# A two-block transformer kernel on one core: three activation tensors that TensorE reads as moving operands start 32, 224 and 96 bytes further on in SBUF

## The reference

```python
# first block, once
u = rmsnorm(h); q, k, v, g_ret, lru_in, lru_gate, gate_a, gate_b = split(u @ w_in)
y_ret = (silu(g_ret) * retention(q, k, v)) @ w_branch_ret
r = rg_lru(causal_conv(lru_in), ...)              # the recurrence
y_lru = (gelu(lru_gate) * r) @ w_branch_lru
h = h + (sigmoid(gate_a) * y_ret + sigmoid(gate_b) * y_lru) @ w_out
h = h + (silu(g) * up) @ w_ffn_out; h = rmsnorm(h)
# second block, once
o_gla, o_dsa, o_mem = gated_linear_attention(..), sparse_attention(..), memory_attention(..)
merged = gate0 * (o_gla @ w_o_gla) + gate1 * (o_dsa @ w_o_dsa) + gate2 * (o_mem @ w_o_mem)
x = x + merged @ w_out
x = x + hierarchical_moe(rmsnorm(x))
```

## The kernel before

| product | moving, its start | stationary, its start | distance |
|---|---|---|---|
| lru, dsaT, memoT, ret, normedT by weights, 256 columns | 64 | 128 | 192 |
| xT by weights, 256 columns | 64 | 128 | 192 |
| glaT by weights, 256 columns | 192 | 128 | 64 |
| xT by weights, 272 columns | 0 | 128 | 128 |
| weights by mixed, 512 columns | 128 | 128 | 0 |
| weights by hidden, 512 columns | 128 | 64 | 64 |
| pick by zrows, 256 columns | 64 | 64 | 0 |
| normedT by the small weights swhi and swlo, 256 columns, slice k | 64 | 96 and 224, plus 432 k | changes with k |

## Time and profile before

### The profile page before, as it was taken

One profiled execution on the slowest core, in us unless ns is written; L12 is line 12 of the kernel. 1 busy time (PEld: TensorE's weight loads), 2 busy tenths in 40 slices (PEclk: granted clock), 3 DMA queues, 4 the chain that ended last, 5 costly groups with the idle time before them and its releaser, 6 DMA issues.

```text
span 1092.3 us, 17231 instructions
## 1 busy us (share of the span) xinstructions
PE 1078.8 (99%) x7088; PEld 965.0 (88%) x7088; DVE 730.3 (67%) x817; ACT 625.7 (57%) x751; POOL 48.6 (4%) x43
## 2 busy tenths in 40 slices
PE   9999999999999999999999999999999999999997
PEld 7998889999889999998898768899999978888885
DVE  6944675865765454455775649975454778998885
ACT  7653369664465444444574446855444567877773
POOL 0600100000000000000000000000000000000140
PEclk9999999999999999999999999999999999999999
DMA  8552254654646555554446333253446547999991
GB/s 312 194 193 77 79 193 155 249 192 141 249 159 222 199 192 187 196 193 155 157 170 213 116 116 129 103 193 116 168 166 220 200 186 259 331 374 350 340 347 78
DMA packets 30786, 214.84 MB, mean 197 GB/s; under 512 B 3424, under 2 KB 3680, under 8 KB 5248
## 3 DMA queue, kind: packets, MB, share of 16 engines
q1 hardware_dynamic: 28400, 199.35, 51.3%
q0 software_dynamic: 1904, 13.14, 3.2%
q10 hardware_dynamic: 416, 1.40, 0.3%
HBM read 212.82 MB, written 1.05 MB: 196 GB/s over the span
## 4 chain that ended last, share of the span: by engine, by line
PE 95%; DVE 3%; ACT 1%; DMA 0%; issue 0%; DVEq 0%; SPq 0%; ACTq 0%
PE bank L565 28%; PE bank L567 28%; PE bank L566 28%; PE bank L626 2%; PE bank L1037 1%; PE bank L1114 1%; PE bank L959 1%; PE bank L941 1%; DVE wlo L1690 1%; DMA buf<-x_dram 0%; PE bank L707 0%; PE bank L872 0%; PE bank L1091 0%; PE bank L704 0%; PE bank L868 0%
## 5 line engine op out<-in xcount | busy, mean ns | idle before, releaser
L1690 DVE TENSOR_TENSOR wlo<-raw,whi 128x2048 fp32r<-128x2048 f32 x138 | 317.8, 2307 | 168.0 <-ACT whi L1149 167.7
L1149 ACT ACTIVATE whi<-raw 128x2048 fp32r<-128x2048 f32 (+1 forms) x168 | 319.3, 1906 | 131.0 <-PE bank L567 127.2
L565 PE MATMUL bank<-normedT_hi,whi 128*128 128x256 f32 x640 | 177.6, 278 | 0.0
L566 PE MATMUL bank<-normedT_lo,whi 128*128 128x256 f32 x640 | 177.0, 277 | 0.0
L567 PE MATMUL bank<-normedT_hi,wlo 128*128 128x256 f32 x640 | 177.0, 277 | 0.0
L1149 ACT ACTIVATE buf<-bank 128x512 f32<-128x512 f32 (+5 forms) x147 | 71.0, 526 | 156.0 <-PE bank L567 127.2
L565 PE MATMUL bank<-xT_hi,whi 128*128 128x256 f32 (+1 forms) x448 | 127.1, 284 | 0.8 <-issue 0.8
L566 PE MATMUL bank<-xT_lo,whi 128*128 128x256 f32 (+1 forms) x448 | 126.4, 282 | 0.0
L567 PE MATMUL bank<-xT_hi,wlo 128*128 128x256 f32 (+1 forms) x448 | 126.4, 282 | 0.0
L565 PEld LDWEIGHTS bank<-normedT_hi,whi 128*128 128x128 f32 x640 | 120.1, 188 | 1.0 <-issue 0.6
L566 PEld LDWEIGHTS bank<-normedT_lo,whi 128*128 128x128 f32 x640 | 120.3, 188 | 0.7 <-issue 0.2
(11 more groups left out here) (406 smaller groups left out, 2260.1 us busy)
## 6 DMA issues: line engine op xcount, KB each, us to landing
raw<-weights_dram SPq DMA_DIRECT2D x168, 1024.0 KB, 4.9
buf<-weights_dram SPq DMA_DIRECT2D x19, 1024.0 KB, 6.9
buf<-x_dram SPq DMA_DIRECT2D x2, 512.0 KB, 4.4
buf<-mem_dram ACTq DMA_DIRECT2D x1, 1024.0 KB, 8.9
out_dram<-buf SPq DMA_DIRECT2D x4, 256.0 KB, 2.7
buf<-final_w_dram POOLq DMA_DIRECT2D x1, 512.0 KB, 4.1
con<-consts_dram SPq DMA_DIRECT2D x1, 486.0 KB, 9.3
buf<-small_w_dram SPq DMA_DIRECT2D x1, 432.0 KB, 11.8
```

Of the source, the lines that this page charges most:

```text
L565: E.matmul(out_, lh, rh, start=start, stop=False)
L566: E.matmul(out_, lh, rl, start=False, stop=False)
L1149: return S.activation(out_, in_, func, **kw)
L1690: V.tensor_tensor(wlo[:, n % SLOTS, :], raw[:, n % SLOTS, :], whi[:, n % SLOTS, :].bitcast(f32), sub).then_inc(piece_split, 1)
```

## The change

Each of the three pairs gets an offset `at`. lru starts 8 elements (32 bytes) further on, dsaT 56 elements (224 bytes), memoT 24 elements (96 bytes), hi and lo alike. Their starts modulo 256 become 96, 32 and 160, and the distances 224, 160 and 32, which are 7, 5 and 1 times 32. The buffers have 2176 elements and the tensors 2048, so the shifted tensors stay in their buffers. No instruction is added, removed or moved on any engine: the sequences of all five engines are the same in both programs, and so is every shape. The instructions that write these tensors and those that read them take other addresses.

```diff
@@ -369,7 +369,7 @@
         RG, IG, TH, AA, A2, HS = cols(7, TM), cols(9, TM), cols(8, TM), cols(10, TM), cols(11, TM), cols(7, TM)
-        LT, LTP = cols(13), pair("lru", 10, 11)
+        LT, LTP = cols(13), pair("lru", 10, 11, at=HELD // 2)
         GA, GB, RTP = cols(4), cols(5), pair("ret", 6, 7)
@@ -406,11 +406,11 @@
-        ODP = pair("dsaT", 9, 10)
+        ODP = pair("dsaT", 9, 10, at=3 * HELD + HELD // 2)
         MQR, MQT = rows(11), cols(12)
         MP = buf[8][:, 0:2048].rearrange("p (a c) -> p a c", a=4)
         MPT = buf[13][:, 0:2048].rearrange("p (h s t) -> p h s t", h=MH, s=2)
-        OMP = pair("memoT", 11, 12)
+        OMP = pair("memoT", 11, 12, at=HELD + HELD // 2)
```

## The result

The changed kernel takes 1096.79 us (median of 17 runs, 1094.47 to 1098.65); the kernel before, 17 runs beside them, takes 1094.1 us (1091.94 to 1095.14). The ratio is 1.0026, with a 95% interval of 1.0018 to 1.0035: 2.8 us slower, 2.0 to 3.8. The forecast was +2.6 us, given as 1095.9 us on the 1093.3 us of the first three runs, with a range of 1090.4 to 1097.6; on the 1094.1 us of the 17 runs it would be 1096.7.

What follows compares the result with a forecast made beforehand. TensorE was taken as the bound, busy 1078.8 of 1092.3 us. The terms 0 + 2.6 + 0 + 0 gave +2.6 us on 1093.3 us, so 1095.9 us (+0.24%), range 1090.4 to 1097.6.

Steps and rivals of the forecast that it cites:

- Step 1: 576 matmuls of lru, dsaT and memoT: streaming from the new distances costs 4.5 ns each, 2.6 us; chance 0.37.
- Stays at 113: Rival: the three stages keep 113 ns despite the new distances; 1093.3 us, 0.0%; chance 0.28.
- A start in the middle of 64 bytes costs extra: Rival for the changed matmuls: 120 to 121 ns each, +3.9 to +4.5 us; chance 0.19 for 119 ns and more.
- Faster: Rival: new starts avoid a clash of reads in the 576 matmuls; 2.7 to 3.7 us gained; chance 0.16, 0.08 over 3.3 us.
- The estimate of 109.2 ns: Skill's N/2.4 + 2.5 ns between 256-column matmuls, set beside the faster side; 2.3 us less if the new starts reached it.
- The skill's rule of two independent ports: TensorE reads moving operand and weight load through separate SBUF ports, so the change would be worth 0.
- Step 2: ScalarE and VectorE writing at the new starts: any change covered by 43, 78 and 75 us before TensorE reads; 0.
- Step 3: Stages behind move as a block, charged 0; gate2 keeping the slower pace would be 0.9 us more.

Runs made afterwards that it cites:

- Run 1: Kernel before plus 25 groups of 48 matmuls, 256 columns, at chosen distances between moving and stationary start; 1247.99 us, which measures nothing.
- runs 2 to 4: Changed kernel with distances exchanged, with even multiples, or with dsaT back at 192; 1098.26, 1096.19 and 1093.82 us, kernel before 1095.21.
- run 7: Kernel before plus groups with one column loaded repeatedly, 32 loaded columns, or 128 moving columns, at several distances; no total given, it is no measure.
- no_dsa: Changed kernel with dsaT put back to distance 192, lru and memoT still changed; 1093.82 us, one execution, kernel before 1095.21.
- paces_512: Kernel before plus 16 groups of 48 matmuls with 512 moving columns at the eight distances; no total given, it is no measure.
- entries: Kernel before plus groups at each distance, each followed by two at 192, then transposes followed by a group at 192; no total given.
- even: Changed kernel with even multiples: lru at distance 128, dsaT at 64, memoT at 0; 1096.19 us, one execution, kernel before 1095.21.
- turned_round: Changed kernel with distances exchanged: lru 160, dsaT 32, memoT 224; 1098.26 us, one execution, kernel before 1095.21.
- weights32: Kernel before with the weights' parts whi and wlo moved by 32 bytes, activations left alone; 1115.1 us against 1093.63, ratio 1.0192.
- best: Kernel before with hidden and memT products at distance 0 and one bf16 matmul ahead of gb.3 and br_lru; 1098.96 us against 1093.91, ratio 1.0044.
- hidden_0: Kernel before with hidden alone moved to distance 0; 1097.88 us against 1093.9, ratio 1.0037.

## Why the prediction was right

**Step 1, streaming from the new starts (+2.6 us).** Right in its mechanism and nearly in its size. The price was 4.5 ns, to 117.7, taken from ret, gla and gate0; the three stages measure 118.3, 117.3 and 116.7, mean 117.4, which over 576 matmuls is 2.4 us. Run 1 found the same three numbers with nothing else of the kernel in them, and runs 2 to 4 moved them between tensors. The prediction's own sentence, that right in kind and wrong in being one number is possible, applies. That the price came so near is in part luck: ret and gate0 lie at 192 and show its second pace, 117.8, which is no price of another distance. Of the three only gla is one.

**The rivals.** "Stays at 113" fell in all three stages. "A start in the middle of 64 bytes costs extra" fell in run 1, where moving both starts by 32 bytes changed nothing; its 120 ns belong to distances 0 and 96 and to the second pace of 128. The 120 ns that the small weights showed at 32 and 160, with 88 loaded columns and over a few matmuls, are 116.7 and 117.3 with 128 columns. "Faster" fell: 113.3 is the floor of every table for 256 columns. The estimate of 109.2 ns from the Trainium skill ("TensorE: Matmul & The Clock Gate", "Back-to-back issue gap") was not reached either; that section gives its formula for the gap of an isolated matmul and says that in a stream where each has its own load both set the pace, as they do here, so the estimate was no forecast for this stream. The skill's rule of two independent ports ("TensorE: Matmul & The Clock Gate", "Step-by-step: what each phase is for") would have made the change worth nothing; the runs decide against it here, for what is loaded (run 7: 113.3 or 116.7 ns at distance 192) and from where (run 1: 118.3 or 113.3 ns for the same moving start) changes the pace of the stream.

**Step 2, writing (0).** Right. The profile after has 2292, 682 and 692 ns for the lo parts, the durations of the earlier trace rows.

**Step 3, the stages behind (charged 0).** Wrong in that profile by the 0.9 us it named: gate2 kept a slower pace, 117.8, and *no_dsa* took that away again. It rested on the earlier trace rows, where 113 ns came back within three matmuls behind distance 64. That was one hand-over, not a rule; behind dsaT at 160 it didn't come back.

**Why the total still fits.** Step 1 was 0.2 us too high and step 3 0.8 us too low, so the nearness of +2.6 and +2.8 is luck as well. The steps measured add to 0.94 + 0.77 + 0.84 + 0.65 = 3.2 us, and the times show 2.8 (2.0 to 3.8). A part of the difference may be that lru's 113.3 before is itself a draw: of eight profiles in which it lies at 192 with nothing put ahead of it, two had it at 117.8 (*paces_512*, *entries*), so its mean price is (6 x 0.94 + 2 x 0.12) / 8 = 0.74 and the sum 3.0. That is worked out from eight profiles and not measured.

**What scatters the times.** One part is ret, which was at 117.8 in ten of the 13 profiles that have it at 192 and at 113.3 in three (the changed kernel, *even*, *paces_512*): 1 us. A larger part is the granted clock. Of the 17 executions of the changed kernel the four with a mean granted clock of 0.997 took 1097.4 to 1098.7 us, and the three with 1.0 took 1095.1 to 1096.2. Where a profile has such a stretch it is short and early. The windows from 100 to 140 us of the kernel before and of *turned_round*, whose 1098.26 us it lengthened:

```profile
100.00:140.00 40.00, 40.00 (x253) 33.80 (x253) 25.13 (x50) 17.81 (x33) 9.86 (x8) 1.00 0.23 79
```

```profile
100.00:140.00 40.00, 40.00 (x241) 33.30 (x240) 24.65 (x49) 16.41 (x32) 8.87 (x8) 0.92 0.23 79
```

It doesn't make the 2.8 us: beside the 21 executions of the kernel before that are on record with a granted clock of 0.997 to 1.0 (they ran beside *weights32*, *best* and *hidden_0*), the changed kernel is slower by 2.3 to 3.1 us on average at each of these clocks.

**Open.** Which physical thing the two reads clash on, and why 196 is so much worse than 192, no run shows. What sets the state was not found: a late start turned it once in 13 profiles; behind transposes it was the slow one six times of six in *entries*, and lru, behind transposes as well, is mostly fast. And why 160 leaves gate2 slow in the kernel but a group fast, with 64 the other way round, stays open; the groups differ from the stages in reading one slot over and over and in having no hi and lo in turn, and neither was tried.

## What to carry to other kernels

Where TensorE is the bound, read the starts of matmuls and compare stages of the same shape: 113 against 118 ns is invisible in the page and was worth 21 us where nearly every product changed. Before moving a tensor in SBUF, measure a table of distances between the moving and the stationary start for the shape that will run, since the best for 256 columns (192) is not that for 512 (0), and then time the whole kernel, because a stage can hand its pace to those behind it. Single profiles of such a kernel don't rank versions; their stages say what changed, and repeated times say whether it matters.

## What was not expected of the hardware

- For fp32r matmuls with a 128-column load each, the pace depends on the distance between the two operands' starts modulo 256 bytes: 113.3 to 120.0 ns in steps of 32 bytes, 123.3 at 196, for 256 moving columns; 226.7 to 234.2 for 512; 111.7 at all eight for 128.
- At distance 192 the same instructions run at 113.3 or at 117.8 ns, mostly hold it through whole stages (18 pieces, 864 matmuls, in *hidden_0*), and take it over from the stage ahead; one late start turned it inside a stage of *entries*. Distances 160 (117.3 or 118.7) and 128 (118.6 or 120.0) have two paces as well.
- A smaller load (32 columns, or one column repeated) does not remove the extra time; it moves it to other distances: 192 goes from 113.3 to 116.7 with one column repeated, and 128 from 118.6 to 113.3.
